# Other token blocks, another DMA model in the order planner, and first weight chunks halved by rows, in a two-layer decoder kernel on 8 cores

## The chip, the cores and the metric

The kernel runs on all 8 NeuronCores of one Trainium2 chip. Each core takes one prompt sequence (2048 tokens) and 16 of the 128 sample sequences (8 tokens each, 128 tokens in all), through both layers; nothing passes between cores. The weights are the same for all cores and each core reads them in f32 from HBM. The metric is the time on the device, in microseconds (us), of the slowest core. Engines: PE multiplies, ACT evaluates functions and copies, DVE does elementwise work, POOL does some of it and issues the weight DMAs, SP issues the other DMAs.

## The reference

Each layer normalises the tokens, multiplies them by one wide input matrix, and feeds three branches:

```python
hn = rms_norm(h, norm_mix)
proj = hn @ w_in
q, k, v, g_out, g_lr, xp, u, vv, gates = jnp.split(proj, offs, axis=-1)
g_log = log_sigmoid(g_lr @ w_gk2 + b_gk) / 16            # A: gated linear attention (GLA), 4 heads
o, s_new = gla_mix(q, k, v, g_log, s_gla, chunk)          # S_t = diag(a_t) S_{t-1} + k_t v_t ; o_t = q_t S_t
branch_a = (rms_norm(o, gla_norm) * silu(g_out)) @ w_br_a
branch_b = pool_mix(xp, ...) @ w_br_b                     # B: trailing means over 2, 4, 8, 16 tokens
branch_c = (gelu(u) * (tril(W_s) gelu(vv) + b)) @ w_br_c  # C: spatial gate in chunks of 128
h = h + (sigmoid(ga)*branch_a + sigmoid(gb)*branch_b + sigmoid(gc)*branch_c) @ w_out
h = h + relu(rms_norm(h) @ w_ff1)**2 @ w_ff2
```

D_MODEL is 1024, D_FF 4096; the outputs are the final-normed tokens, the GLA states, the pooling histories and the new v rows.

## The kernel before

**Tiles and blocks.** The 2176 tokens of a core are 17 tiles of 128. Tile 0 holds the sample tokens, tiles 1 to 16 the prompt. `BLK` (line 24) groups them in five blocks, here of 3, 3, 3, 4 and 4 tiles. A product with a weight chunk that is held feature-major (`hn_fm`, line 738) streams a whole block, so one matmul has 384 or 512 columns; one that is held token-major (`proj_tm`, `vgrp`) has a tile as the stationary operand and streams weight columns.

**Weight chunks.** The matrices come as chunks of 1024 x 512 (2 MB of f32 in HBM, 1 MB of bf16 in SBUF), in the fixed list `order`: v0, v1, k, q, g0, g1, xp, u, vv, and so on, through a ring `wring` of 7 slots. `wload` (line 651) issues them from POOL. The first two chunks, v0 and v1, come in two halves each, with semaphores of their own (`first`), and layer 0's `vgrp` starts on a half.

**Start.** x tiles come through three buffers `xt`, from SP. For each, ACT sums the squares (`xj`) and takes ln and exp for the root, DVE scales into `xn`, PE transposes, and DVE copies into `hn` (`norm_to_hn`, line 757). From tile 6 on, the load of x waits for chunk g0 (`after=[slots[4]]`).

**Stages.** In each layer: projections, gate and scan of the GLA branch block by block (`gla_project`, `gla_gate`, `gla_scan`), with the work on the 16 sample states cut into four portions by `yield` (line 990) and one portion after each of the first blocks; then pooling and spatial gate (`mix_block`), gated merge (`gate_block`), output projection (`out_block`), and the feed-forward net (`ff1`, `ff2`).

**ACT's tables.** Exp and ln share one table set; silu, gelu and sigmoid have one each (`SETS`, line 32). A switch shows in the profile as ACT_TABLE_LOAD.

**The order.** Nothing runs in the order of the code. Each operation is recorded as a node with a cost; `lay_out` (line 247) is a list scheduler that places nodes on five engines by its own clock, picks by start time and rank, and gives each PSUM tile a bank. DMA transfers end by a model of their own (`dma_at`). The instructions are then written in that order, and each engine runs its list strictly in turn. What the model believes of a duration changes only the order; the chip decides the times.

## Time and profile before

| | us |
|---|---|
| median of 3 runs | 2383.77 (2382.52 to 2385.54) |
| the profiled execution, its own time | 2381.28 |
| its span on the slowest core (core 5) | 2380.2 |
| spans of the other cores | 2371.6 to 2379.2 |
| PE busy | 2323.0 |
| DVE, ACT, POOL busy | 1273.8, 886.3, 245.9 |

The page divides the span into 40 slices of 59.5 us: PE is at 6 and 8 tenths in the first two and at 9 or more from the third to the last but one. The granted clock of PE averages 0.998 of full speed on this core. The GLA stages of the two layers lie at about 68 to 316 us and 1225 to 1480 us, and there ACT and DVE are at their busiest.

### The profile page before, as it was taken

What the parts mean: (1) busy time and instruction counts of PE and PEld (TensorE: products, weight loads), DVE (VectorE), ACT (ScalarE), POOL (GpSimd) and SP (SyncE); (2) the same over time, 40 slices, a digit from 0 to 9 for tenths busy, and PEclk for the clock granted to TensorE, in tenths of its full rate; (3) what the DMA queues carried; (4) which work ended last, traced back from release to release, by engine and by line L of the source; (5) the groups of instructions that cost most, each with busy time, mean ns of one, the idle gap of its engine ahead of it and who ended that gap; (6) DMA issues with size and microseconds to landing.
All of it is one profiled execution on the core that took longest, in us unless ns stands there. A gap on an engine that the chain in (4) does not pass through costs nothing.

```text
span 2380.2 us, 40912 instructions; the slowest of 8 cores (2371.6 to 2380.2 us)
## 1 busy us (share of the span) xinstructions
PE 2323.0 (98%) x13392; PEld 1236.5 (52%) x13392; DVE 1273.8 (54%) x2231; ACT 886.3 (37%) x1810; POOL 245.9 (10%) x266
## 2 busy tenths in 40 slices
PE   6899999999999999999999999999999999999998
PEld 4576555546445454545455555564554454545453
DVE  3787776444465444434567776744434644434355
ACT  3877753222233121212456678322222421211133
POOL 2123222000000000000012233200000000000000
PEclk9999999999999999999999999999999999999999
DMA  9554936154186040406492467451815642222112
GB/s 162 143 165 122 186 125 142 71 97 111 70 159 103 1 72 1 76 1 116 127 164 74 149 137 157 100 135 63 142 72 107 126 65 36 36 37 36 18 59 93
DMA packets 219415, 229.41 MB, mean 96 GB/s; under 512 B 54315, under 2 KB 203307, under 8 KB 216106
## 3 DMA queue, kind: packets, MB, share of 16 engines
q0 software_dynamic: 83584, 78.45, 23.8%
q1 hardware_dynamic: 135626, 148.35, 20.9%
q8 instruction: 113, 1.85, 0.3%
q14 instruction: 92, 0.75, 0.1%
HBM read 240.41 MB, written 55.05 MB: 124 GB/s over the span
## 4 chain that ended last, share of the span: by engine, by line
PE 91%; DVE 3%; issue 2%; ACT 2%; DMA 2%; POOL 0%; DVEq 0%; ACTq 0%; SPq 0%; POOLq 0%
PE ps L454 90%; DMA wring<-w_in 1%; PE ps L467 1%; DVE U L428 0%; DMA Sf<-sgla 0%; DVE Sf L428 0%; ACT rsg L417 0%; DVE tmp L428 0%; ACT L417 0%; ACT tmp L417 0%; DVE sqg L425 0%; DVE lv L815 0%; ACT Sb L417 0%; DVE pt L425 0%; ACT xj L417 0%
## 5 line engine op out<-in xcount | busy, mean ns | idle before, releaser
L454 PE MATMUL ps<-hn,wring 128*128 128x384 bf16 (+1 forms) x6400 | 1245.4, 347 | 7.8 <-DVE sgt L425 1.7
L454 PEld LDWEIGHTS ps<-hn,wring 128*128 128x128 bf16 x6400 | 621.6, 98 | 545.4 <-issue 13.4
L454 PE MATMUL ps<-wring,a 128*128 128x512 bf16 x2176 | 476.0, 379 | 0.2 <-DVE a L425 0.2
L417 ACT ACTIVATE rl<-ps 128x384 f32<-128x384 f32 (+1 forms) x320 | 169.9, 532 | 637.9 <-PE ps L454 522.2
L425 DVE TENSOR_TENSOR h<-h,ps 128x512 f32<-128x512 f32 x340 | 233.1, 687 | 277.1 <-PE ps L454 276.1
L454 PEld LDWEIGHTS ps<-wring,a 128*128 128x128 bf16 x2176 | 212.8, 98 | 255.1 <-issue 0.7
L425 DVE TENSOR_TENSOR a<-rl 128x384 bf16<-128x384 f32 (+1 forms) x320 | 194.9, 612 | 276.0 <-ACT rl L417 268.0
L417 ACT ACTIVATE sg<-ps 128x384 f32<-128x384 f32 (+1 forms) x240 | 127.9, 533 | 450.3 <-PE ps L454 322.3
L454 PE MATMUL ps<-wring,hn 128*128 128x256 bf16 (+1 forms) x1088 | 193.7, 330 | 12.2 <-DMA wring<-w_in 10.8
L425 DVE TENSOR_TENSOR tmp<-sg,ps 128x384 f32<-128x384 f32 (+1 forms) x160 | 97.3, 608 | 154.4 <-ACT sg L417 79.1
L454 PEld LDWEIGHTS ps<-wring,hn 128*128 128x128 bf16 x1088 | 105.2, 99 | 79.3 <-issue 15.3
L454 PE MATMUL ps<-OBs,wring 128*128 128x384 bf16 (+1 forms) x640 | 143.8, 347 | 0.0
L675 POOL DMA_DIRECT2D wring<-w_ff x32 | 28.0, 875 | 1047.2 <-PE ps L454 1047.2
L425 DVE TENSOR_TENSOR acc<-sg,ps 128x384 f32<-128x384 f32 (+1 forms) x80 | 48.5, 607 | 162.7 <-PE ps L454 162.7
L454 PE MATMUL ps<-H4s,wring 128*128 128x384 bf16 (+1 forms) x640 | 130.7, 347 | 0.0
L454 PE MATMUL ps<-wring,mg 128*128 128x512 bf16 x544 | 119.7, 379 | 0.0
L425 POOL TENSOR_TENSOR go<-tmp,go 128x512 bf16<-128x512 f32 x64 | 77.8, 1221 | 244.4 <-DVE tmp L428 213.0
L417 ACT ACT_TABLE_LOAD x71 | 91.1, 1283 | 26.4 <-PE ps L454 24.2
L454 PEld LDWEIGHTS ps<-H4s,wring 128*128 128x128 bf16 x640 | 62.5, 98 | 55.7 <-issue 0.3
L454 PEld LDWEIGHTS ps<-OBs,wring 128*128 128x128 bf16 x640 | 62.6, 98 | 55.0
L454 PEld LDWEIGHTS ps<-wring,mg 128*128 128x128 bf16 x544 | 52.8, 98 | 61.3
L428 DVE SCALAR_TENSOR_TENSOR tmp<-ps,vec_t,rsg 128x256 f32<-128x256 f32 x136 | 61.7, 477 | 28.6 <-ACT rsg L417 27.5
(137 smaller groups left out, 1777.6 us busy)
## 6 DMA issues: line engine op xcount, KB each, us to landing
wring<-w_ff POOLq DMA_DIRECT2D x32, 1024.0 KB, 13.1
wring<-w_in POOLq DMA_DIRECT2D x28, 1024.0 KB, 16.1
Sf<-sgla SPq DMA_DIRECT2D x64, 256.0 KB, 3.7
gla_s<-Sf SPq DMA_DIRECT2D x64, 256.0 KB, 2.8
H4s<-H_d SPq DMA_DIRECT2D x12, 768.0 KB, 8.5
OBs<-OB_d SPq DMA_DIRECT2D x12, 768.0 KB, 5.0
h_d<-h SPq DMA_DIRECT2D x17, 512.0 KB, 2.7
h<-h_d SPq DMA_DIRECT2D x17, 512.0 KB, 9.9
```

Source lines behind the costliest of these rows:

```text
L417: op(ACT, lambda: nc.scalar.activation(out=now(out), in_=now(in_), func=func, **kw), reads, writes, occ, 125.0, SETS.get(func))
L425: op(E, lambda: E.e.tensor_tensor(out=now(out), in0=now(in0), in1=now(in1), op=alu), reads, writes, occ, 90.0)
L428: op(DVE, lambda: nc.vector.scalar_tensor_tensor(out=now(out), in0=now(in0), scalar=scalar, in1=now(in1), op0=op0, op1=op1), reads, writes ...
L454: inst = nc.tensor.matmul(now(m[0]), m[1], m[2], start=m[3], stop=m[4], **kw)
L467: inst = nc.tensor.transpose(now(o), i, ident_ap)
L675: nc.gpsimd.dma_start(out=view, in_=src).then_inc(slot_sem[k], 16)
```

## The change

The kernel after has the blocks 4, 3, 4, 3, 3. The halves of v0 and v1 are cut by rows (four of the eight groups of 128 rows, all 512 columns) instead of by columns (all rows, 256 columns): a half product adds half of the sum into the same PSUM tile. Both chunks are issued ahead of the two small weights `wglr` and `wgk2`; `wglr` comes from HBM already padded to 32 columns, so that its memset is gone. The loads of `bsp` and `rep` follow tile 5 of `hn`; one more x tile (tile 6) is loaded without waiting for g0. The portions of the samples end at states 8, 18 and 28 instead of 6, 16 and 26. The product of the pooling weights (`fuse`) is recorded inside the first gate block rather than ahead of it. The planner's DMA model now lets the transfers of both queues progress together, at 300 and 265 bytes per ns, and frees what waits for a transfer when it lands by that model.

```diff
 NTILE = 17
-BLK = [(0, 3), (3, 3), (6, 3), (9, 4), (13, 4)]
+BLK = [(0, 4), (4, 3), (7, 4), (11, 3), (14, 3)]
...
     w_gk2 = din("w_gk2", [DEPTH, 128, 512])
-    w_glr = din("w_glr", [DEPTH, 128, KT, 16])
+    w_glr = din("w_glr", [DEPTH, 128, KT, 32])
...
-        dma_at = [4000.0] * 5
+        clock = 4000.0
+        coming = []
+        moving = {3: collections.deque(), 4: collections.deque()}
+        landing = []
...
                     best = pick
+            upto = best[1] if best is not None else 1e12
+            while clock < upto and (coming or moving[3] or moving[4]):
+                on = [(moving[3], 3.0 if moving[4] else 1.0), (moving[4], 1.5 if moving[3] else 1.0)]
+                on = [(q, r) for q, r in on if q]
+                to = min([upto] + [clock + q[0][1] * r for q, r in on] + ([max(clock, coming[0][0])] if coming else []))
+                for q, r in on:
+                    q[0][1] -= (to - clock) / r
+                    if q[0][1] < 1e-6:
+                        m = q.popleft()[0]
+                        landing.append((to + m.lat, m.idx))
+                        landing.sort()
+                clock = to
+                while coming and coming[0][0] <= clock:
+                    _, i, e, work = coming.pop(0)
+                    moving[e].append([nodes[i], work])
+                if landing and landing[0][0] < upto:
+                    upto = landing[0][0]
+            if landing and landing[0][0] <= upto:
+                at, i = landing.pop(0)
+                free_up(nodes[i], at)
+                continue
...
             if n.byts:
-                at0 = max(dma_at[e], s + occ)
-                other = dma_at[7 - e]
-                work = n.byts / (290.0 if e == 3 else 150.0 if dma_at[4] < 20000.0 else 245.0)
-                both = max(0.0, other - at0)
-                dma_at[e] = at0 + (both + work - both / 2 if work > both / 2 else work * 2)
-                fin = dma_at[e] + (3500.0 if e == 3 else 2500.0)
+                coming.append((s + occ, n.idx, e, n.byts / (300.0 if e == 3 else 265.0) + 100.0))
+                coming.sort()
...
                 n *= s
-            if turn:
-                n *= 3
-            record(self.E, fn, reads, writes, 500.0 if self.E is SP else 900.0, 0.0, byts=n, after=after)
+            record(self.E, fn, reads, writes, 1250.0 if turn else 500.0 if self.E is SP else 900.0,
+                   2000.0, byts=n, after=after)
...
     hH = [[part(hB[t], 0, 2 * KB), part(hB[t], 2 * KB, 2 * KB)] for t in range(NTILE)]
-    mkb = [24, 30, 36, 42, 50]
+    mkb = [24, 32, 38, 46, 52]
...
             for i in range(2):
-                c = slice(256 * i, 256 * i + 256)
-                plq.dma(vs[0][:, :, c], todo[0][1][:, :, c], writes=[first[2 * n + i]])
+                c = slice(4 * i, 4 * i + 4)
+                plq.dma(vs[0][:, c, :], todo[0][1][:, c, :], writes=[first[2 * n + i]])
...
             release((slot_sem[k], 16 * slot_cnt[k]), rs, ws)
-        record(POOL, fn, (), [b] + (first[2 * k:2 * k + 2] if n in (NSLOT, NSLOT + 1) else []), 900.0 * len(todo), 0.0, byts=byts)
+        record(POOL, fn, (), [b] + (first[2 * k:2 * k + 2] if n in (NSLOT, NSLOT + 1) else []), 900.0 * len(todo), 2000.0, byts=byts)
...
         act(ssq[7].t[:, :], ssq[7].t[:, :], AF.Ln, [ssq[7]], [ssq[7]])
-        memset(wglr.t[:, :, :], 0.0, [wglr])
...
     def gla_consts(l):
-        plq.dma(wglr.t[:, :, 0:16], w_glr[l], writes=[wglr])
+        plq.dma(wglr.t[:, :, :], w_glr[l], writes=[wglr])
             ts(wpm.t[:, g, :], wpm.t[:, g, :], vec_t.t[:, V_PSC + l * 4 + g:V_PSC + l * 4 + g + 1], ALU.mult, [wpm, vec_t], [wpm])
-        spq.dma(bsp.t[:, :, :], b_sp[l:l + 1].broadcast_to([128, 4, 128]), writes=[bsp], after=[slots[6]])
+        spq.dma(bsp.t[:, :, :], b_sp[l:l + 1].broadcast_to([128, 4, 128]), writes=[bsp], after=[hnB[5]])
         plq.dma(wsT.t[:, :, :], w_spT[l].rearrange("g s t -> s g t"), writes=[wsT], after=[slots[6]])
-        spq.dma(rep.t[:, :], rep_d[l], writes=[rep], after=[slots[6]])
+        spq.dma(rep.t[:, :], rep_d[l], writes=[rep], after=[hnB[5]])
...
                 for i in range(2):
-                    c = slice(256 * i, 256 * i + 256)
-                    pe_group([(ps.t[:, c], hn_v(b)[:, kt, j * 128:(j + 1) * 128], view[:, kt, c], kt == 0, kt == KT - 1, True)
-                              for kt in range(KT)], [first[2 * hf + i], hnB[BLK[b][0] + j]], [ps])
+                    pe_group([(ps.t[:, :], hn_v(b)[:, kt, j * 128:(j + 1) * 128], view[:, kt, :], kt == 0, kt == KT - 1, True)
+                              for kt in range(4 * i, 4 * i + 4)], [first[2 * hf + i], hnB[BLK[b][0] + j]], [ps])
...
                 spq.dma(gla_s[l, i, 2 * hp:2 * hp + 2].rearrange("h d e -> d h e"), s.t[:, :, :], reads=[s])
-                if n in (5, 15, 25):
+                if n in (7, 17, 27):
...
         ga, ba, gb, bbc, gc = [wget(l, "%s%d" % (nm, hf)) for nm in ("ga", "ba", "gb", "bbc", "gc")]
-        if b == 0:
-            for g in range(4):
-                ps = psum()
-                pe_group([(ps.t[:, :], wpm.t[:, g, :], bbc[1][:, g, :], True, True)], [wpm, bbc[0]], [ps])
-                act(bbc[1][:, g, :], ps.t[:, :], AF.Copy, [ps], [bbc[0]])
+        def fuse(g):
+            ps = psum()
+            pe_group([(ps.t[:, :], wpm.t[:, g, :], bbc[1][:, g, :], True, True)], [wpm, bbc[0]], [ps])
+            act(bbc[1][:, g, :], ps.t[:, :], AF.Copy, [ps], [bbc[0]])
                 m = hf * 4 + m4
+                if b == 0 and pi == 0 and m4 > 1:
+                    fuse(2 * m4 - 4)
+                    fuse(2 * m4 - 3)
...
         for t in tiles(b):
-            norm_to_hn(t, hB[t].t[:, :], hH[t], hj, hx[t % 2], turn=b >= 2)
+            norm_to_hn(t, hB[t].t[:, :], hH[t], hj, hx[t % 2], turn=t > 5)
...
     for t in range(NTILE):
-        if t == 6:
+        if t == 7:
             wget(0, "g1")
-        spq.dma(xt[t % 3].t[:, :], rows(x_p, x_s, t), writes=[xt[t % 3]], after=[slots[4]] if t > 5 else ())
+        spq.dma(xt[t % 3].t[:, :], rows(x_p, x_s, t), writes=[xt[t % 3]], after=[slots[4]] if t > 6 else ())
...
                 act(wn.t[:, i * 512:(i + 1) * 512], wps[i].t[:, :], AF.Copy, [wps[i]], [wn])
-            wget(0, "v0")
+            wget(0, "v1")
...
     gk2 = gk2.reshape(DEPTH, 128, 512)
-    glr = np.ascontiguousarray(f(w_in)[:, :, C_GLR:C_GLR + 16].reshape(DEPTH, KT, 128, 16).transpose(0, 2, 1, 3))
+    glr = np.zeros((DEPTH, 128, KT, 32), np.float32)
+    glr[:, :, :, 0:16] = f(w_in)[:, :, C_GLR:C_GLR + 16].reshape(DEPTH, KT, 128, 16).transpose(0, 2, 1, 3)
     shared = {
```

**PE at the start**, from the first product with v0 on. xn are tiles being transposed. dq_pl0 to dq_pl5 are the POOL queue's first transfers in the order of issue: before, v0's halves, wglr, wgk2, v1's halves; after, v0's halves, v1's halves, wglr, wgk2. Before:

```order
L454 MATMUL ps<-wring,hn 128x256 [waits dq_pl0,sem_dve]
L454 MATMUL ps<-wring,hn 128x256 x7
L467 MATMUL ps<-ident_bf,xn_71 128x128 [waits sem_dve]
L467 MATMUL ps<-ident_bf,xn_71 128x128 x7
L454 MATMUL ps<-wring,hn 128x256 [waits sem_dve]
L454 MATMUL ps<-wring,hn 128x256 x7
L467 MATMUL ps<-ident_bf,xn_70 128x128 [waits sem_dve]
L467 MATMUL ps<-ident_bf,xn_70 128x128 x7
L454 MATMUL ps<-wring,hn 128x256 [waits dq_pl1]
L454 MATMUL ps<-wring,hn 128x256 x15
L454 MATMUL ps<-hn,wglr 32x384 [waits dq_pl2,sem_dve]
L454 MATMUL ps<-hn,wglr 32x384 x7
```

After:

```order
L480 MATMUL ps<-wring,hn 128x512 [waits dq_pl0,sem_dve]
L480 MATMUL ps<-wring,hn 128x512 x3
L480 MATMUL ps<-wring,hn 128x512 [waits dq_pl1]
L480 MATMUL ps<-wring,hn 128x512 x3
L493 MATMUL ps<-ident_bf,xn_71 128x128 [waits sem_dve]
L493 MATMUL ps<-ident_bf,xn_71 128x128 x7
L480 MATMUL ps<-wring,hn 128x512 [waits dq_pl2]
L480 MATMUL ps<-wring,hn 128x512 x3
L480 MATMUL ps<-wring,hn 128x512 [waits sem_dve]
L480 MATMUL ps<-wring,hn 128x512 x11
L493 MATMUL ps<-ident_bf,xn_70 128x128 [waits sem_dve,sem_act]
L493 MATMUL ps<-ident_bf,xn_70 128x128 x7
```

Tile 0 now takes both halves of v0 before tile 1 is transposed, and a product with the first half of v1 (dq_pl2) stands ahead of tile 1's own products.

**ACT in the GLA stage of layer 0**, at the gate of the first block that it works on with 512 columns after block 0; go are silu results, rsg needs ln and exp. Before:

```order
L417 ACTIVATE tmp_0_96<-ps 128x512
L417 ACTIVATE go_78<-ps 128x512 x2
L417 ACTIVATE rsg_98<-ps 128x256
L417 ACTIVATE rsg_98<-rsg_98 128x256
L417 ACTIVATE go_78<-ps 128x512 x2
L417 ACTIVATE tmp_1_97<-ps 128x512
L417 ACTIVATE Sb_90<-U_86,eblP 128x256
L417 ACTIVATE Sb_91<-U_87,eblP 128x256
L417 ACTIVATE go_78<-ps 128x512
L417 ACTIVATE tmp_0_96<-ps 128x512
L417 ACTIVATE rsg_99<-ps 128x256
L417 ACTIVATE rsg_99<-rsg_99 128x256
```

After:

```order
L443 ACTIVATE rsg_98<-ps 128x256
L443 ACTIVATE rsg_98<-rsg_98 128x256
L443 ACTIVATE go_77<-ps 128x512 x2
L443 ACTIVATE Sb_90<-U_86,eblP 128x256
L443 ACTIVATE Sb_91<-U_87,eblP 128x256
L443 ACTIVATE tmp_1_97<-ps 128x512
L443 ACTIVATE Sb_92<-U_88,eblP 128x256
L443 ACTIVATE Sb_93<-U_89,eblP 128x256
L443 ACTIVATE tmp_0_96<-ps 128x512
L443 ACTIVATE go_77<-ps 128x512 x6
L443 ACTIVATE rsg_99<-ps 128x256
```

Before, the silu results come in twos and ones with rsg between them; after, six of them stand in one row.

## Rows read from the trace of the kernel before

**Rows 1.** First two lines of the page, core 5: engine, busy us, share.

```profile
span 2380.2 us, 40912 instructions; the slowest of 8 cores (2371.6 to 2380.2 us)
...
PE 2323.0 (98%) x13392; PEld 1236.5 (52%) x13392; DVE 1273.8 (54%) x2231; ACT 886.3 (37%) x1810; POOL 245.9 (10%) x266
```

**Rows 2.** Busy time by stage; columns PE, PEld, DVE, ACT, POOL, clock, DMA share, GB/s.

```profile
30.00:43.00 13.00, 8.15 (x60) 6.03 (x58) 4.54 (x8) 6.72 (x19) 0.00 (x0) 0.74 1.13 151
68.00:125.00 57.00, 50.14 (x417) 33.59 (x415) 42.11 (x74) 47.55 (x115) 7.35 (x6) 1.00 0.52 147
125.00:250.00 125.00, 118.44 (x1051) 82.23 (x1049) 103.43 (x240) 95.43 (x188) 43.44 (x51) 1.00 0.51 139
250.00:316.00 66.00, 63.11 (x432) 36.12 (x430) 48.83 (x106) 51.39 (x101) 20.94 (x21) 1.00 0.86 169
1225.00:1480.00 255.00, 244.17 (x1753) 141.57 (x1752) 184.45 (x417) 189.92 (x380) 69.41 (x74) 1.00 0.54 125
```

**Rows 3.** Waits of PE: total us, times, longest.

```profile
PE ps L454 <- DMA wring<-w_in: 10.8, 3, 4.9
```

**Rows 4.** PE in order of time, 14 to 60 us: start, length, operation.

```profile
17.73 1.86 PE L454 MATMUL ps<-wring,hn 128*128 128x256 bf16 x8 [4.67 <-DMA wring<-w_in]
...
24.47 1.91 PE L454 MATMUL ps<-wring,hn 128*128 128x256 bf16 x16 [1.27 <-DMA wring<-w_in]
...
36.43 5.16 PE L454 MATMUL ps<-wring,hn 128*128 128x256 bf16 x24 [4.85 <-DMA wring<-w_in]
...
41.87 3.66 PE L454 MATMUL ps<-wring,hn 128*128 128x256 bf16 x32
45.37 0.61 PE L467 MATMUL ps<-ident_bf,xn 128*128 128x128 bf16 x8
...
51.05 5.36 PE L454 MATMUL ps<-hn,wring 128*128 128x384 bf16 x32
```

**Rows 5.** DMA, 20 to 25 us.

```profile
DMA packets 1672, 1.11 MB, mean 223 GB/s; under 512 B 967, under 2 KB 1482, under 8 KB 1672
...
q0 software_dynamic: 1450, 0.34, 77.3%
```

**Rows 6.** DMA, 28 to 34 us.

```profile
DMA packets 1669, 1.21 MB, mean 201 GB/s; under 512 B 298, under 2 KB 1570, under 8 KB 1668
...
q0 software_dynamic: 1163, 0.62, 82.1%
```

**Rows 7.** DMA, 50 to 60 us.

```profile
q0 software_dynamic: 1524, 1.53, 111.8%
```

**Rows 8.** Instructions on tile xt, 0 to 140 us: duration ns min/median/max.

```profile
L417 ACT ACTIVATE xj<-xt x17: 1039/1055/1074, 5.6 to 113.4; 128x1024 bf16<-128x1024 f32 x17
L417 ACT ACTIVATION_READ_ACCUMULATOR xj<-xt x17: 185/187/219, 6.5 to 114.3; 128x1 f32 x17
L428 DVE SCALAR_TENSOR_TENSOR xn<-xt,ssq,wn x17: 1273/1280/1286, 10.6 to 120.0; 128x1024 bf16<-128x1024 f32 x17
```

**Rows 9.** DVE in order of time: the copy of a transposed tile.

```profile
31.52 0.69 DVE L437 COPY hn<-ps 128x1024 bf16<-128x1024 bf16 x1 [2.91 <-PE ps L467]
```

**Rows 10.** SP queue in order of time, 0 to 130 us.

```profile
3.99 0.47 SPq L379 DMA_DIRECT2D bsp_p<-b_spatial  x1
```

**Rows 11.** ACT groups, 68 to 316 us: busy us, mean ns, idle before.

```profile
L417 ACT ACT_TABLE_LOAD x31 | 39.8, 1283 | 7.2 <-PE ps L454 6.8
```

**Rows 12.** ACT groups, 1225 to 1480 us.

```profile
L417 ACT ACT_TABLE_LOAD x32 | 41.1, 1283 | 15.6 <-PE ps L454 15.2
```

**Rows 13.** Line L417 over the whole span.

```profile
L417 ACT ACT_TABLE_LOAD  x71: 1283/1283/1283, 1.3 to 1856.7; - x71
```

**Rows 14.** Chain that ended last: shares by line, then two of its pieces.

```profile
by line: PE ps L454 89.9%; issue 2.1%; DMA wring<-w_in 1.3%; PE ps L467 0.7%; DVE U L428 0.4%; DMA Sf<-sgla 0.4%; DVE Sf L428 0.3%; ACT rsg L417 0.3%; DVE tmp L428 0.3%; ACT L417 0.3%; ACT tmp L417 0.3%; DVE sqg L425 0.2%; DVE lv L815 0.2%;
...
42.04 3.49 PE ps L454 x32
...
699.47 1.73 PE ps L454 x8
```

More of the change, by code:

```diff
@@ L1 @@
+import collections
 import numpy as np
@@ L270, in lay_out, with free_up @@
                 ready[num[id(n.E)]].append(n)
-        for _ in range(len(nodes)):
+        def free_up(n, fin):
+            for m in n.succ:
+                j = m.idx
+                t = fin + 250.0 if n.E is not PE or m.E is not PE else fin - n.lat
+                if t > rdy[j]:
+                    rdy[j] = t
+                need[j] -= 1
+                if need[j] == 0:
+                    ready[num[id(m.E)]].append(m)
+        while len(order) < len(nodes):
             while oldest < len(tiles_in_order) and id(tiles_in_order[oldest]) in opened:
@@ L336, in lay_out @@
             order.append(n)
-            for m in n.succ:
-                j = m.idx
-                t = fin + 250.0 if e != 0 or m.E is not PE else fin - n.lat
-                if t > rdy[j]:
-                    rdy[j] = t
-                need[j] -= 1
-                if need[j] == 0:
-                    ready[num[id(m.E)]].append(m)
+            if not n.byts:
+                free_up(n, fin)
         return max(free), order, kof
```

## The prediction

> **What bounds the kernel now.** I read the page's busy shares first [rows 1]: PE is busy for 2323.0 of 2380.2 us. The change touches no product's size, only when it runs, so what can be won is PE's idle time and what PE loses inside its busy time. The table by stage [rows 2] shows where that lies. PE idles 57 - 50.1 = 6.9 us from 68 to 125 us, 6.6 from 125 to 250, 2.9 from 250 to 316, and 10.8 in layer 1's GLA stage. That is 16.3 us in layer 0's stage and 27.1 in both; ACT is busy for 47.6 of 57 us in the first of these stretches. The rest is the start. PE's waits [rows 3] put 10.8 us there on three waits for chunks of w_in, and PE's own order of time [rows 4] shows them: v0's first half at 17.7 us, v1's first half at 36.4. From 41.9 us on PE runs without a gap to 68.
>
> **The start.** What must arrive ahead of v1's first half gets smaller, and I price it per packet. From 28 to 34 us, when the POOL queue moves halves by columns, its 1163 packets took 82.1% of 16 x 6 = 96 us: 67.8 ns each, and 0.62 MB / 1163 is about 512 B [rows 6]. From 50 to 60 us, with whole chunks, 1524 packets took 111.8% of 160 us: 117.4 ns for 1024 B [rows 7]. A half by columns is 1024 packets, 69.4 us of engine time or 4.34 us over 16 engines; by rows it is 512 packets, 60.1 us or 3.76. Three halves save 1.7 us. w_glr was 1024 packets of 32 B: from 20 to 25 us 1450 packets took 77.3% of 80 us, and if the 483 that are not under 512 B cost 67.8 ns, the other 967 cost 30 ns [rows 5]; so w_glr is 1.9 us. w_gk2 is 128 packets of 1024 B, 0.9 us. Both now come behind v1. bsp (0.26 MB, issued at 4.0 us [rows 10]) now comes after tile 5; at the 201 GB/s of [rows 6] 1.3 us. The masks (0.17 MB) wait for tile 2, which comes later, 0.8. x tile 5 (0.52 MB, 2.6 at that rate) is asked for some 4 us later; I take 0.6 of it. Sum: 7.2 us, so v1's first half lands at 36.4 - 7.2 = 29.2 us.
>
> The trace agrees only in part with the Trainium skill (DMA: Bandwidth & Descriptors, Specifications), which says that transfers of 512 B and more already run at line rate. By that rule the cut by rows gives nothing, v1 lands 1.7 us later than I say, and the predicted time is 1.7 us higher. The packets above cost 0.132 ns per byte at 512 B and 0.115 at 1024 B, so I go by them.
>
> PE's list, though, gives much of this back. After v1's first half lands it runs: 16 products of 512 columns; the transposes of tile 2 and their copy; 8 and 12 products; tile 3's transposes; 4 products; wglr; 8 products. A product costs 216 ns at full clock (8 in 1.73 us) [rows 14]. PE has by then stood idle, as before 36.4 us, where 24 products of 256 columns took 5.16 us, 215 ns each against 3.49 / 32 = 109 [rows 4, 14], with a granted clock of 0.74 over 30 to 43 us [rows 2]: the lower level, 1.2 GHz, after 5 us of waiting. I let 8 of the 16 run at it: 8 x 0.43 + 8 x 0.216 = 5.2 us. The transposes and copy are 0.5 + 0.7 [rows 9], 20 products 4.3, transposes 0.5, 4 products 0.9, wglr 0.4, 8 products 1.7: 14.2, with 0.3 for waits between. That is a state 0.3 us of work short of what the kernel before has reached at 45.4 us (52 products' worth of 512 columns there, 56 here, but two sets of transposes and gates fewer). So the start breaks even if v1 lands at 45.4 - 14.8 = 30.6, and gains 1.4 us at 29.2. Bounds: with packets and w_gk2 alone (2.6 us) it loses 3.2; with all of x tile 5 out of the way (9.2 us) it gains 3.4. I take 1.4, since nearly all of the 7.2 has rows.
>
> ACT and DVE stand behind PE here: ACT now copies v of tile 0 before it sums tile 2's squares, and v of tile 1 before tile 3's. Tile 3's chain (1.06 + 0.19 + 0.5 on ACT, 1.28 on DVE [rows 8]) starts when tile 1's product is done, about 3.5 us after v1's landing, and ends near 8.5, while its transposes stand at 10.8. It is covered by 2 us. From k on the chunks are not late: PE reaches k's first product near 50 us, and before it found k there at 51.05 without a wait [rows 4].
>
> **The GLA stages.** A table load costs ACT 1283 ns, and there are 71 [rows 13], 31 in layer 0's stage and 32 in layer 1's [rows 11, 12]. I counted, in ACT's list of each kernel, the changes between the sets of exp/ln, silu, gelu and sigmoid. Before gives 71, the trace's number. After gives 52: 14 fewer in layer 0, 5 fewer in layer 1, because silu results stand together in longer runs. That is 24.4 us less on ACT. What PE gets of it: on the chain that ended last, ACT's table loads are 0.3% of 2380, 7.1 us for 71, or 0.1 us each [rows 14]; 19 give 1.9. From above: if all of PE's idle time in these stages came from loads, 14 x 16.3/31 + 5 x 10.8/32 = 9.1. Below, an order in which other operations take the place of the loads gives 0. I take 3.0, nearer to the chain, since it is the row that follows releases.
>
> One x tile more (tile 6) is normed before the crowded stretch: 11 were normed there with 6.9 us of idle PE, so 0.6. PE's halves: 272 products of 512 columns stand for 544 of 256: 272 x (2 x 109 - 216) = 0.5.
>
> **Edits at nothing.** wglr's memset ran on DVE before the first x arrived. The fuse products, the yields, `mkb` and the turn rule keep their counts (tiles 6 to 16 are turned as before); they lie in stretches where PE is full. h of tile 16 now shares space with block 2 and 3 of the merge and is loaded 2 tiles ahead instead of 3, 2 x 16 x 0.216 = 6.9 us before use; its adds wait on DVE and PE has free PSUM banks. The blocks keep their number, and three of 384 columns and two of 512 stay. The last block is of 3 tiles, which shortens only ACT's 0.6 us step there. As bounds for all reordering beside the loads I keep 4 us either way, 15% of the 27.1.
>
> **Sum.** 1.4 + 3.0 + 0.6 + 0.5 = 5.5 us off the profiled execution's 2381.3 gives 2375.8. The median of the runs is 2.5 above that execution, so 2383.8 - 5.5 = 2378.3 us.
>
> **Rivals.** A measurement tells 0.2%, 4.8 us, from no change.
> A, the forecast: 2 to 9 us faster, 2375 to 2382. Chance 0.50, of which 0.30 beyond the bound.
> B, the table loads count nearly in full: ACT is over 80% busy from 68 to 125 us [rows 2], and waits on it pass to PE through DVE. 9.1 for 3.0, and 2 more at the start: 13.6 faster, 2370. Against it: the chain holds few loads. 0.18.
> C, nothing: v1 lands at 30.6 and ACT's saved time turns into waits for PE. The trace shows ACT's loads already preceded by 15.6 us of idling in layer 1 [rows 12]. 0.5 + 0.6 = 1.1 faster, 2382.7. 0.19.
> D, slower: PE's clock. The waits for v0's second half and v1's first stand close together, and PE has 4 products and one set of transposes between them. If it stays at 1.2 GHz through all 48 products behind v1's landing, 40 more than I count, that costs 40 x 0.216 = 8.6 us; with the loads at their lower bound: -1.4 - 1.1 + 8.6 = 6.1 slower, 2389.9. It decides from 34 of the 40 on. For it: the 24 products at 36.4 us all ran low. Against it: the next 32, from 41.9 us, all ran at full clock [rows 4]. 0.13.
> That the change doesn't do what it says has no place beside the counted loads and packets.
>
> The likeliest is A, 2378.3. The range 2367 to 2387 holds A and C, most of B, and the better edge of D. Faster 0.30 + 0.18 = 0.48, the same 0.20 + 0.19 = 0.39, slower 0.13.
>
> **What the profile after would show.** POOL packets of 1024 B from the start; PE's first product on v1 at 28 to 31 us, and tile 4's transposes near 44; 52 table loads; PE's idle time in the two GLA stages down from 27 to about 24 us; a granted clock at the low level for 2 to 4 us around 30 us. I am wrong if v1 lands after 32 us, if PE waits on k or q, or if the GLA stages idle as before with 19 loads fewer.

## The result, and the profile after

The kernel after takes 2397.2 us (median of 5 runs, 2392.9 to 2398.0), that of before 2383.8 (5 runs, 2380.9 to 2385.5): the ratio is 1.005, 95% interval 1.0036 to 1.0063. The forecast was 2378.3, with 2367 to 2387 as its range and 0.13 for slower: the measured time lies 10 us above the range. In some executions cores of one die run at a lower clock, whatever the kernel; the ratios leave these out, except for one execution of a_turn3 (2414.5 us), one of a_nudge (2411.5) and two of b_blkyield (2415.7 and 2423.7), without which theirs are given too.

The profiled execution took 2398.0 us; its slowest core is core 0. First the head of its page, to be held against [rows 1]:

```profile
span 2397.0 us, 40156 instructions; the slowest of 8 cores (2381.0 to 2397.0 us)
...
PE 2321.9 (97%) x12948; PEld 1212.1 (51%) x13120; DVE 1277.8 (53%) x2230; ACT 861.6 (36%) x1791; POOL 247.6 (10%) x266
```

PE is as busy as before, and stands idle for 75.1 us where it was 57.2. (Part of that is not idling: 172 matmul records are missing from this core's trace, as 12948 stand beside 13120 weight loads.) Busy time also hides something, which the table by stage shows in its clock column (core 0; columns as in [rows 2]):

```profile
30.00:43.00 13.00, 11.12 (x67) 5.33 (x70) 4.64 (x5) 7.78 (x19) 0.00 (x0) 1.00 1.12 200
68.00:125.00 57.00, 50.84 (x386) 29.70 (x387) 48.06 (x88) 45.92 (x115) 9.89 (x8) 0.96 0.54 135
125.00:250.00 125.00, 117.34 (x874) 67.59 (x883) 98.54 (x219) 88.53 (x180) 39.35 (x46) 1.00 0.43 125
250.00:316.00 66.00, 54.88 (x359) 31.74 (x360) 40.57 (x94) 42.67 (x95) 20.98 (x21) 0.90 1.07 203
1225.00:1480.00 255.00, 245.14 (x1711) 140.35 (x1731) 181.22 (x406) 185.34 (x382) 68.11 (x74) 1.00 0.62 133
```

From 250 to 316 us PE idles 11.1 us for 2.9, and the granted clock averages 0.90 for 1.00. Before, it had been 1.00 in every stretch from 68 us on.

One core is one sample, so I took the same stretches on all eight. This table is worked out from them: the mean of PE's idle time, and of what the clock cost (the stretch times one minus its mean granted clock), in us.

| stretch | before: idle, clock | after: idle, clock | change |
|---|---|---|---|
| 0 to 68 us | 17.3, 2.1 | 19.2, 0.7 | +0.5 |
| 68 to 380, to the end of layer 0's mixing | 17.0, 0.0 | 18.9, 6.2 | +8.1 |
| 740 to 860, output projection, then ff1 and ff2 | 0.1, 0.0 | 2.7, 0.8 | +3.4 |
| 1225 to 1540, the same mixing in layer 1 | 11.2, 0.0 | 8.7, 0.0 | -2.5 |
| 1900 to 2360, layer 1's feed-forward | 0.7, 0.0 | 2.6, 0.0 | +1.9 |

The sum is +11.4 us; the mean span of the eight cores went from 2376.0 to 2387.3. So the table leaves nothing large out, and the loss has two places: layer 0's mixing, mostly by PE's clock, and the two feed-forward stages. The clock column has two digits, which makes its products rough: the falls in the trace itself, 3.4 or 6.8 us each at 0.50, add up to 5.6 us for the 6.2. And it misses something in the first row of the table: up to a core's first clock record (20 to 27 us before, 22 to 31 after) it says 1.00 while 4 products of 512 columns take 1.86 us, 465 ns each, half speed. Estimated as half of PE's busy time up to there, this cost 5.2 us before and 6.1 after.

**The start** brought v1 earlier than forecast. PE of core 0 in order of time, beside [rows 4]:

```profile
15.69 1.86 PE L480 MATMUL ps<-wring,hn 128*128 128x512 bf16 x4 [3.23 <-DMA wring<-w_in]
21.98 1.86 PE L480 MATMUL ps<-wring,hn 128*128 128x512 bf16 x4 [4.43 <-DMA wring<-w_in]
...
25.92 3.61 PE L480 MATMUL ps<-wring,hn 128*128 128x512 bf16 x16 [1.22 <-DMA wring<-w_in]
...
31.24 4.26 PE L480 MATMUL ps<-wring,hn 128*128 128x512 bf16 x19 [1.26 <-ACT ssq L443]
...
39.85 0.61 PE L493 MATMUL ps<-ident_bf,xn 128*128 128x128 bf16 x8 [0.50 <-DVE xn L454]
...
45.47 1.89 PE L480 MATMUL ps<-hn,wring 128*128 128x512 bf16 x8
```

v1's first product is at 25.9 us, not 29.2. The 16 products take 3.61 us here, 226 ns each, which is full clock; on the other seven cores they take 5.3 to 6.1 us. Core 1 of the same execution, and core 2 of the kernel before, which [rows 4] (core 5) should be held against:

```profile
25.92 5.62 PE L480 MATMUL ps<-wring,hn 128*128 128x512 bf16 x16 [3.97 <-DMA wring<-w_in]
```

```profile
30.39 2.78 PE L454 MATMUL ps<-wring,hn 128*128 128x256 bf16 x24 [2.76 <-DMA wring<-w_in]
```

Before, PE's first product with v1 was at 30.4 to 36.4 us, by core, 32.9 in the mean; core 5 was the last. Now it is at 24.9 to 26.4, 25.8 in the mean. ACT loads as many tables as counted, 52 for 71:

```profile
L443 ACT ACT_TABLE_LOAD x52 | 66.7, 1283 | 32.6 <-PE ps L480 30.6 <-DVE ssq L467 1.3
```

**The clock.** The largest single wait of core 0, and what follows it; first PE in order of time, then the table by stretches:

```profile
257.12 1.46 PE L480 MATMUL ps<-hn,wring 128*128 128x384 bf16 x8
...
264.68 0.24 PE L480 MATMUL ps<-kqS,Sinb 128*128 128x8 bf16 x4 [5.99 <-POOL Sinb L463]
...
265.19 2.76 PE L480 MATMUL ps<-hn,wring 128*128 128x384 bf16 x8
...
268.07 6.56 PE L480 MATMUL ps<-hn,wring 128*128 128x384 bf16 x32
```

```profile
258.00:262.00 4.00, 0.69 (x5) 0.23 (x3) 1.78 (x4) 2.28 (x7) 0.00 (x0) 1.00 1.03 168
262.00:266.00 4.00, 1.32 (x9) 0.85 (x10) 0.43 (x2) 0.00 (x0) 1.72 (x2) 0.71 1.12 201
266.00:270.00 4.00, 4.00 (x15) 1.78 (x13) 3.07 (x8) 1.54 (x4) 1.15 (x2) 0.50 1.08 224
270.00:274.00 4.00, 4.00 (x25) 2.36 (x24) 3.53 (x6) 1.33 (x3) 2.03 (x3) 0.94 1.02 286
```

Eight products of 384 columns take 1.46 us ahead of the wait and 2.76 behind it. The clock column shows 0.50, the 1.2 GHz level; the engine had stood nearly idle for six us. "PE busy" says 4.00 of 4.00 us there: a fall of the clock is invisible in busy shares. The wait is paid a second time behind itself. It also happened without a long wait: core 1 has only waits of 0.4 to 1.1 us, but five of them from 284 to 292 us, and then PE runs at the low level:

```profile
284.00:288.00 4.00, 2.95 (x26) 1.58 (x23) 2.98 (x7) 1.99 (x7) 2.27 (x2) 1.00 1.09 156
288.00:292.00 4.00, 1.49 (x13) 0.84 (x13) 2.83 (x9) 3.81 (x10) 0.00 (x0) 1.00 1.14 160
292.00:296.00 4.00, 2.99 (x13) 1.85 (x14) 1.43 (x4) 3.21 (x9) 2.31 (x2) 0.60 1.12 158
296.00:300.00 4.00, 4.00 (x12) 1.53 (x11) 2.01 (x4) 2.30 (x8) 0.95 (x1) 0.54 1.13 210
```

**The feed-forward stages.** Before, PE waited for nothing between 740 and 860 us. Now it waits for DVE's squares `a`. Three rows of DVE, two views of SP's queue (732 to 738 us and 750 to 755), and one row of PE, all of core 0:

```profile
761.91 1.28 DVE L454 SCALAR_TENSOR_TENSOR hx<-h,ssq,wn 128x1024 bf16<-128x1024 f32 x1 [4.62 <-DMA hn<-hx]
763.11 1.29 DVE L451 TENSOR_TENSOR a<-rl 128x512 bf16<-128x512 f32 x2
768.28 1.28 DVE L454 SCALAR_TENSOR_TENSOR hx<-h,ssq,wn 128x1024 bf16<-128x1024 f32 x1 [3.88 <-DMA hn<-hx]
```

```profile
L406 SPq DMA_TRANSPOSE hn<-hx x2: 1231/1232/1232, 732.5 to 734.3; - x2
...
DMA to landing us min/median/max: 3.0/3.0/3.0
```

```profile
L406 SPq DMA_TRANSPOSE hn<-hx x2: 1238/2760/4282, 751.4 to 753.5; - x2
...
DMA to landing us min/median/max: 10.4/12.6/14.7
```

```profile
771.73 0.81 PE L480 MATMUL ps<-wring,a 128*128 128x512 bf16 x3 [1.67 <-DVE a L451]
```

DVE scales a tile into one of two buffers `hx`, and SP transposes it by DMA into `hn`. DVE can't write the buffer until the transpose has read it. The two transposes of 732.5 and 734.3 us each landed 3.0 us after their issue. Those of 751.4 and 753.5 us, issued while two weight chunks of 1 MB from POOL were under way (issued at 751.2 and 752.9, landed at 761.2 and 768.0), took 10.4 and 14.7 us, and at their landings, 761.8 and 768.2, DVE's two waits above end. DVE's strict order has the scaling ahead of the squares, so the squares stand behind a DMA that they don't need, and PE behind the squares.

### The profile page after: what moved, and what is told of

Its sections match the earlier page's. It is cut to its first block, busy times and chain, and to the rows that moved or that the text cites. A ratio compares the mean times of both kernels' runs of the same rounds, so it can differ in the third digit from the quotient of the medians.

```text
span 2397.0 us, 40156 instructions; the slowest of 8 cores (2381.0 to 2397.0 us)
## 1 busy us (share of the span) xinstructions
PE 2321.9 (97%) x12948; PEld 1212.1 (51%) x13120; DVE 1277.8 (53%) x2230; ACT 861.6 (36%) x1791; POOL 247.6 (10%) x266
## 4 chain that ended last, share of the span: by engine, by line
PE 87%; DMA 5%; DVE 3%; issue 2%; ACT 2%; POOL 1%; SPq 0%; DVEq 0%; ACTq 0%; POOLq 0%
PE ps L480 87%; DMA hn<-hx 1%; DMA Sf<-sgla 1%; DMA wring<-w_in 1%; DMA H_d<-go 1%; PE ps L493 1%; ACT L443 0%; DVE tmp L454 0%; DMA rep<-w8rep 0%; ACT rsg L443 0%; POOL go L451 0%; DVE Sf L454 0%; DVE U L454 0%; DVE xn L454 0%; DVE km L458 0%
## 5 line engine op out<-in xcount | busy, mean ns | idle before, releaser
L480 PE MATMUL ps<-wring,hn 128*128 128x512 bf16 x786 | 185.0, 381 | 13.8 <-DMA wring<-w_in 8.9
L480 PEld LDWEIGHTS ps<-wring,hn 128*128 128x128 bf16 x816 | 77.6, 98 | 98.7 <-issue 17.2
## 6 DMA issues: line engine op xcount, KB each, us to landing
wring<-w_ff POOLq DMA_DIRECT2D x32, 1024.0 KB, 11.2
H4s<-H_d SPq DMA_DIRECT2D x12, 768.0 KB, 5.0
OBs<-OB_d SPq DMA_DIRECT2D x12, 768.0 KB, 5.1
```

Source lines behind the costliest of these rows:

```text
L480: inst = nc.tensor.matmul(now(m[0]), m[1], m[2], start=m[3], stop=m[4], **kw)
```

## The experiments

All kernels below are this kernel with some parts of the change. Beside the ratio to the kernel before I read three numbers from the trace, as means over the eight cores: when ACT does its first gate of `gate_block` in layer 0 (380.9 us before, 389.3 after: "first gate"), the time from the first to the last relu in layer 0's feed-forward (453.8 with the blocks of before, 456.5 with the new ones where nothing waits), and layer 1's first gate to the end (832.5).

**Which part costs?** The start alone, the blocks alone, the planner's DMA model alone, and all but the planner's model:

b_start has the lines of the start (row halves, both chunks first, the padded w_glr, bsp and rep behind tile 5, x tile 6 earlier):

```diff
-                c = slice(256 * i, 256 * i + 256)
-                plq.dma(vs[0][:, :, c], todo[0][1][:, :, c], writes=[first[2 * n + i]])
+                c = slice(4 * i, 4 * i + 4)
+                plq.dma(vs[0][:, c, :], todo[0][1][:, c, :], writes=[first[2 * n + i]])
...
-            wget(0, "v0")
+            wget(0, "v1")
```

> The kernel before with the start of the kernel after alone: row halves, both first chunks ahead of the small weights, the padded w_glr, bsp and rep behind tile 5, x tile 6 loaded without waiting. Blocks, planner, sample portions and fuse are those of before. Theory P (the planner's new DMA model causes the loss) and theory B (the new blocks cause it): 0 to 4 us faster than before, 2380 to 2384 us. Theory S (the start causes it: v1 comes earlier but the rest of the start loses what it gives, and puts DVE's work later): 5 to 13 us slower, 2389 to 2397.

Measured: 1.0028 (1.0016 to 1.0039), first gate at 386.8 us.

b_blocks:

```diff
-BLK = [(0, 3), (3, 3), (6, 3), (9, 4), (13, 4)]
+BLK = [(0, 4), (4, 3), (7, 4), (11, 3), (14, 3)]
...
-    mkb = [24, 30, 36, 42, 50]
+    mkb = [24, 32, 38, 46, 52]
```

> The kernel before with the blocks 4, 3, 4, 3, 3 alone, with the places in SBUF of the merge buffers that go with them. Theory B (a first block of four tiles crowds DVE from 80 to 125 us, where it went from 33.7 to 42.4 us busy of 45, and PE's clock falls there): 8 to 13 us slower, 2392 to 2397 us. Theory P and theory S: within 3 us of before.

Measured: 1.0156 (1.0137 to 1.0175), first gate at 398.8, and 21.8 us more between the two first gates.

b_plan has all lines on the planner's DMA model; a_oldplan is the kernel after without them:

```diff
-                dma_at[e] = at0 + (both + work - both / 2 if work > both / 2 else work * 2)
-                fin = dma_at[e] + (3500.0 if e == 3 else 2500.0)
+                coming.append((s + occ, n.idx, e, n.byts / (300.0 if e == 3 else 265.0) + 100.0))
+                coming.sort()
...
-            if turn:
-                n *= 3
-            record(self.E, fn, reads, writes, 500.0 if self.E is SP else 900.0, 0.0, byts=n, after=after)
+            record(self.E, fn, reads, writes, 1250.0 if turn else 500.0 if self.E is SP else 900.0,
+                   2000.0, byts=n, after=after)
```

> The kernel before with the planner's new DMA model alone. Theory P (it takes a DMA transpose for a cheap transfer, puts DVE's work that waits for one too early, and plans the landings of state and weights too early): 6 to 13 us slower, 2390 to 2397 us, with waits of PE on DVE of 2 to 4 us in the feed-forward stages near 770 and 1930 us. Theory B and theory S: within 3 us of before.

Measured: 1.0147 (1.0130 to 1.0164), first gate at 404.4, feed-forward 460.7 for 453.8, last part 839.0 for 832.5.

> The kernel after with the planner's DMA model of before; the blocks, the start, the portions and the fuse are those of after. Theory P: the loss goes, 2378 to 2385 us, below before. Theory B or S: it stays, 2392 to 2398 us. If the parts only work together (theory M: any new order loses or wins by chance some us), this lies between.

Measured: 1.0069 (1.0054 to 1.0084), first gate at 394.4; the feed-forward stages run as if nothing waited (456.4, 832.0).

Each of the three parts alone costs, two of them three times as much as all together. (The later fuse and the sample portions were not run alone.) Each theory of one guilty part falls. Only the feed-forward waits follow a part, the planner's model.

**The transpose's price, and the other parts undone one by one.**

a_turn3 is the kernel after with one line changed; a_oldblk and a_oldstart are the kernel after without the lines of b_blocks and of b_start.

```diff
-                   2000.0, byts=n, after=after)
+                   2000.0, byts=3 * n if turn else n, after=after)
```

> The kernel after; alone the planner again counts the bytes of a DMA transpose three times, as before (issue and delay stay as after). Theory P1 (the planner takes the transposes of the feed-forward stage for too cheap and puts the scaling of the next tile ahead of the squares that PE waits for): PE's waits on DVE at about 760 to 775 and 1930 us go, 2.4 + 0.9 us in the first and 2.0 in the last stage, so the ratio to the kernel before falls from 1.005 to about 1.003 (2391 to 2393 us). Rival (any change of the planner's numbers shuffles the whole order): the stages ahead of 380 us change too, by up to 8 us either way.

Measured: 1.0051, with a wide interval (1.0021 to 1.0081); without the execution of 2414.5 us 1.0023, which is what the theory had. The trace is clear: feed-forward 456.5 for 460.0, last part 832.4 for 835.0, the first gate 1.1 us later (390.4), mean span 2382.6 for 2387.3. The mean of the cores' spans lies at 2381.7 to 2383.5 in the four other executions, and at 2385.0 to 2387.3 in all five of the kernel after.

> The kernel after with the blocks 3, 3, 3, 4, 4 and their buffers of before; start, planner, portions and fuse are those of after. Theory B (blocks of four tiles first bring the fall of PE's clock): the ratio to before falls below 1.002. Theory F (the parts are fitted to each other: each alone cost 3 to 37 us, together 12): it rises to 1.010 to 1.016, like the planner alone.

Measured: 1.0103 (1.0087 to 1.0118).

> The kernel after with the start of before (halves by columns, small weights between the first two chunks, bsp and rep behind g0's slot, one x tile fewer). Theory S (the start costs what b_start showed, 0.28%): the ratio to before falls from 1.005 to 1.002. Theory F: it rises, to 1.007 or more.

Measured: 1.0036 (1.0022 to 1.0051). k's first product comes 4.6 us later than in the kernel after (54.3 for 49.7, by DVE's copy of its result), and yet the first gate is 3.8 us earlier (385.5).

b_blkyield is b_blocks and:

```diff
-                if n in (5, 15, 25):
+                if n in (7, 17, 27):
```

> The kernel before with the new blocks and the new ends of the sample portions. Theory F in its plainest form: a first block of four tiles gives its portion of samples more time, and with the portions of before PE waits for the states of the samples (7.3 us on POOL's Sinb at 262 and 301 us with the blocks alone). Then the ratio falls from 1.0156 with the blocks alone to 1.008 or less, and those waits to under 3 us. Rival: the portions do nothing, 1.014 to 1.017.

Measured: 1.0097 (1.0068 to 1.0125), 1.0073 without the executions of 2415.7 and 2423.7 us. The profiled one is that of 2415.7, so I read it without its cores 2 and 3, which stood at 0.98 in the mean. The first gate of the other six is at 398.9, as late as with the blocks alone, and the clock cost 8.3 us from 68 to 380; the gain over the blocks alone came from layer 1.

**Do the two parts add up, and what does any other order cost?** b_rows has the halves by rows, their order and the padded w_glr only. a_turn3_oldstart is a_turn3 with the start of before.

> The kernel after with two parts undone: the planner counts the bytes of a DMA transpose three times, and the start is that of before. If the two parts add up: the transposes gave back 4.8 us of the mean span (2387.3 to 2382.5, the feed-forward waits gone), the start 3.8 us ahead of the first gate (389.3 to 385.5): mean span 2378.7 us, first gate at 385.5, ratio to before 1.000 to 1.003. Theory F (parts only fit together, each change shuffles the whole order): the first gate anywhere from 381 to 393 us. The waits in the feed-forward stages are gone by either.

Measured: 0.9996 (0.9984 to 1.0008), first gate at 383.8, mean span 2375.6. I could have stopped here: two parts undone, the time of before is back.

> The kernel before with the row halves, both first chunks ahead of the small weights and the padded w_glr alone; bsp, rep and the x tiles are loaded as before. What b_start cost (0.28%, first gate at 386.8 us for 380.9, although the first half of v1 came earlier) lies either in bsp, rep and the x tile moved ahead, then this is 0.998 to 1.001, or in what follows the rows (the small weights late, one product group of 512 columns), then it is 1.002 to 1.004 as b_start.

Measured: 1.0030 (1.0019 to 1.0041). k's first product is 1.7 us earlier than before (47.0 for 48.7), the first gate 6.3 us later (387.2).

b_turn1 is the kernel before with two lines less:

```diff
-            if turn:
-                n *= 3
```

> The kernel before; alone the planner no longer counts a DMA transpose three times. Theory P1: PE waits on DVE's squares at about 770 and 1930 us come up here too, some 2 to 5 us each with the clock falling there, and the rest stays as before: ratio 1.002 to 1.005. Rival: the rest of the planner's model is needed for it, then the feed-forward stages idle as before (0.1 and 0.7 us) and the ratio is 1.000.

Measured: 1.0076 (1.0062 to 1.0089). The first gate stayed (380.7). Feed-forward and last part: 461.7 for 453.8, 839.3 for 832.5. The rows that decide it, on core 4 of this kernel, DVE and then PE:

```profile
744.61 0.56 DVE L423 TENSOR_TENSOR a<-rl 128x384 bf16<-128x384 f32 x1 [0.74 <-ACT rl L415]
755.46 1.28 DVE L426 SCALAR_TENSOR_TENSOR hx<-h,ssq,wn 128x1024 bf16<-128x1024 f32 x1 [10.30 <-DMA hn<-hx]
756.67 1.02 DVE L423 TENSOR_TENSOR a<-rl 128x384 bf16<-128x384 f32 x2
```

```profile
759.86 12.93 PE L452 MATMUL ps<-wring,a 128*128 128x512 bf16 x47 [6.84 <-DVE a L423]
```

The kernel before, DVE at the same place (core 5): more squares stand between the scalings, the buffer is nearly free when its turn comes, and PE waits for none of it.

```profile
746.54 1.28 DVE L428 SCALAR_TENSOR_TENSOR hx<-h,ssq,wn 128x1024 bf16<-128x1024 f32 x1 [0.41 <-DMA hn<-hx]
748.28 0.56 DVE L425 TENSOR_TENSOR a<-rl 128x384 bf16<-128x384 f32 x1 [0.46 <-ACT rl L417]
...
755.29 1.28 DVE L428 SCALAR_TENSOR_TENSOR hx<-h,ssq,wn 128x1024 bf16<-128x1024 f32 x1 [1.25 <-DMA hn<-hx]
```

b_nudge is the kernel before with every landing of a DMA 250 ns later in the model:

```diff
-                fin = dma_at[e] + (3500.0 if e == 3 else 2500.0)
+                fin = dma_at[e] + (3750.0 if e == 3 else 2750.0)
```

> The kernel before; alone each DMA lands 250 ns later in the planner's model, a change with no meaning for the chip. It measures what any other order of the same work costs. Theory F (the order of before is a lucky one of many, and any other loses some us to waits and to falls of PE's clock in layer 0's GLA stage): the first gate comes 3 to 12 us later than at 380.9 us, ratio 1.002 to 1.006, and the clock falls once or twice between 60 and 340 us, where it never did before. If the order of before is ordinary, this lies within 1 us of it.

Measured: 1.0050 (1.0037 to 1.0064), first gate at 390.3; idle 24.5 us and clock 2.3 from 68 to 380. A change that means nothing costs as much as the whole change under study.

**Cost or luck?** If a quarter of a microsecond in the model can do that, no single pair of kernels tells what the start costs. So each was nudged: b_nudge_back by -250 ns, b_rows_nudge, a_turn3_nudge, a_turn3_oldstart_nudge and a_nudge by +250, a_turn3_nudge500 by +500. In the kernels with the new model the line is:

```diff
-                        landing.append((to + m.lat, m.idx))
+                        landing.append((to + m.lat + 250.0, m.idx))
```

> The kernel before; alone each DMA lands 250 ns earlier in the planner's model. A second draw beside the nudge of +250 ns, which cost 0.5%. If the order of before is a lucky one: ratio 1.002 to 1.006 again, the first gate 3 to 12 us after 380.9. If only later landings hurt: 0.998 to 1.001.

Measured: 1.0126 (1.0111 to 1.0141), first gate at 411.1. Waits of PE on core 4, 250 to 400 us, the three longest kinds:

```profile
PE ps L454 <- POOL Sinb L437: 5.4, 2, 3.1
PE ps L454 <- ACT xf L417: 5.3, 2, 5.1
PE ps L454 <- DVE sgt L425: 3.8, 2, 2.5
```

> The kernel before with row halves (as b_rows, 1.003) and the nudge of +250 ns (alone 1.005). If the rows themselves cost 0.3% whatever the order: 1.008. If their cost is that of any other order (luck): they don't add up, 1.000 to 1.006.

Measured: 1.0057 (1.0042 to 1.0072), against 1.0050 with the same nudge without rows.

> The kernel after with transposes counted three times (1.0051 with a wide interval, mean span 2382.5 us) and every landing 250 ns later in the planner's model. If the start of after costs whatever the order: 1.002 to 1.005, and 3 to 5 us above the same nudge with the start of before. If luck: 0.998 to 1.008, with no fixed distance to it.

Measured: 0.9987 (0.9977 to 0.9996), median 2381.1 us. First gate at 378.3. Its feed-forward stages on core 1, and the kernel after's on the same core, 740 to 860 us:

```profile
740.00:860.00 120.00, 120.00 (x605) 58.99 (x603) 51.70 (x80) 22.43 (x43) 3.50 (x4) 1.00 0.36 51
```

```profile
740.00:860.00 120.00, 118.18 (x596) 57.86 (x594) 50.86 (x78) 23.83 (x47) 3.23 (x4) 1.00 0.32 49
```

> The same as a_turn3_oldstart (0.9996), with every landing 250 ns later in the planner's model. If blocks and planner of after are as good as those of before by themselves: 0.998 to 1.002 again. If 0.9996 was a lucky order: 1.002 to 1.006, as the nudge did to before. Below 0.998 it would be a version that beats both kernels.

Measured: 1.0037 (1.0022 to 1.0051), first gate at 387.7.

> The kernel after (transposes cheap, as it is); alone every landing is 250 ns later in the planner's model. With transposes counted three times the same nudge gave 0.9987. If cheap transposes cost 5 us under any order (PE waits on DVE's squares near 760 and 1930 us): 1.0007 to 1.002, with these waits there. If that too belongs to single orders: anything from 0.998 to 1.010, and the waits may be gone.

Measured: 1.0031 (1.0005 to 1.0058), 1.0020 without the execution of 2411.5 us; first gate at 379.0. Its feed-forward (459.9) and last part (835.0) are those of the kernel after; a_turn3_nudge has 456.4 and 832.0.

> The kernel after with transposes counted three times and every landing 500 ns later (0 ns: 1.0051 with a wide interval; 250 ns: 0.9987). If the gain at 250 ns comes with any later landing: 0.997 to 0.9995. If it was one lucky order: 1.001 to 1.007.

Measured: 0.9999 (0.9988 to 1.0011), first gate at 380.9, 45 table loads.

What the pairs say, the ratio with and without each part, all else the same; a_turn3 and a_nudge stand without the executions named:

| part | pairs, with against without | reading |
|---|---|---|
| transposes priced low | after 1.0050 / 1.0023 (mean span 2387.3 / 2382.6); nudged 1.0020 / 0.9987; on before 1.0076 / 1.0000 | costs in every pair: 6.1, 6.5 and 14.7 us in the feed-forward stages |
| the new start | on before 1.0028 / 1.0000; after 1.0050 / 1.0036; with a_turn3 1.0023 / 0.9996; nudged 0.9987 / 1.0037 | +0.28, +0.14, +0.27 and -0.50%: no cost of its own is shown |
| the new blocks | on before 1.0156 / 1.0000; after 1.0050 / 1.0103 | +1.6 and -0.5% |
| the new planner's model | on before 1.0147 / 1.0000; after 1.0050 / 1.0069 | +1.5 and -0.2% |
| row halves | on before 1.0030 / 1.0000; nudged 1.0057 / 1.0050 | +0.3% and +0.07% |
| nudge alone | before: 1.0050 and 1.0126; after: 1.0050 to 1.0020; a_turn3: 0.9987, 0.9999 for 1.0023; a_turn3_oldstart: 1.0037 for 0.9996 | moves the first gate by 4 to 30 us |

## Why the prediction was wrong

**The step that failed** is the one called "Edits at nothing", with its bound: "As bounds for all reordering beside the loads I keep 4 us either way, 15% of the 27.1." I took that bound as a share of PE's idle time, as if a new order could only redistribute what was idle. The nudges show what the same work costs in another order: on the kernel before the first gate moved by 9 us and by 30, where the bound had 4. The kernel before is a good order for its first 380 us: from 68 us to 2360 no core shows a fall of the clock. The kernel after has its first gate 8.4 us later, and with a nudge, all its parts in place, at 379.0, earlier than before.

**In the same step**, "the turn rule keep their counts ... they lie in stretches where PE is full" is wrong in its conclusion. The count of transposed tiles did stay. The diff also takes away `n *= 3`, which stood in front of me as a number that "changes only the order". The order was what kept DVE's squares ahead of a slow DMA. Priced by bytes the transfer of a tile of 256 KB (128 x 1024 of 2 bytes) went from 2.7 us in the model to 1.0. With the model's other terms (1.25 for the issue, 2.0 at the end, the transfer three times as long while POOL's queue moves) a tile beside weights lands 6.2 us after its issue in the new model, and by the line of a_turn3 11.4; on core 0 such tiles took 10.4 and 14.7. So the factor 3 is close where a weight chunk is under way, and too dear for a tile that has the engines to itself: 6.0 in the model of a_turn3, 3.0 measured. That the cheap price makes the waits is shown, in three pairs, and it is the only part of the loss that has a cause in one line: 6.1 us in the mean, of 11.3.

The Trainium skill (Advanced Engine Details and Errata, X-Bar Transpose (TRN2)) says that transposing DMAs are as fast as regular ones, at 350 to 400 GB/s. By that a tile would take 0.7 us, an estimate from the page's figure. This trace does not agree: the lone tile of core 0 that was issued at 732.5 us moved its 256 KB from 733.7 to 735.1, at a mean of 187 GB/s, and the measurement decides.

**The start, +1.4 forecast.** In the mean of the cores the stretch from 0 to 68 us lost 0.5 instead. The landing of v1 was sized well: PE's first product with it is 7.1 us earlier in the mean (25.8 for 32.9) for the 7.2 forecast, and the 16 products behind it took 5.3 to 6.1 us on seven of eight cores, for the 5.2 forecast. What the sum had wrong was the core that it started from: core 5, the last of the eight to get v1. By DVE's copy of k's first result, core 5 gained 3.7 us (49.3 for 53.0) and core 2 lost 5.1 (49.6 for 44.5); the mean went from 48.7 to 49.7. With rows alone k's came 1.7 us earlier, and idle plus clock from 0 to 68 us fell from 19.4 to 17.0 us. But k's first product is not where time is banked: a_oldstart reached it 4.6 us later and the first gate 3.8 us earlier.

**The table loads, +3.0 forecast.** The count was exact, the gain is not there in layer 0. From 68 to 380 us idle plus clock is 17.0 us with 71 loads in the whole kernel (before), 17.5 with 71 (b_turn1), 47.1 with 71 (b_nudge_back), 25.1 with 52 (after), 18.4 with 45 (a_turn3_nudge500), 15.2 with 55 (a_turn3_nudge). There is no order in this. Layer 1's stage did lose 2.5 us of idle time; whether by its fewer loads is open, no run changed the loads alone.

**The rivals.** D came nearest: PE's clock, as a price paid behind clustered waits. It was right in kind: the falls cost 5.6 us in layer 0's mixing, and 5.4 more than before over the whole span, of the 11.3. But I looked for it only at 30 us, where waits for weights stand close. It struck near 66 us on two cores, near 100 on seven, and in layer 0's last blocks on all: at 264 and 305 us on core 0, behind one wait of 6 us and behind shorter ones, and at 292 to 296 on the other seven, behind several of 0.4 to 1.7. B is refuted. The terms of 0.6 and 0.5 us are below what these runs tell apart.

**What stays open.** Which feature makes an order good between 68 and 380 us was not found. Waits for the samples' states (POOL's Sinb, 5.99 us on core 0 and 1.9 in all on core 4 of the same execution) differ from core to core and count by the clock behind them too; no experiment took them away. That a later landing in the model is better in general is not shown either: +250 ns was better for a_turn3 and worse for a_turn3_oldstart and before.

The best of the orders is a_turn3_nudge: 0.9987 (0.9977 to 0.9996) of before, that is the change with the transposes priced three times and one lucky nudge, and it is the lowest of 19 tries.

## What to carry to other kernels

Where a list scheduler writes the order, treat any edit of its costs, or of its nodes, as a fresh draw: nudge a constant two or three times first, and let the range of the forecast, and every verdict on a part, be no narrower than that spread (here 0.2 to 1.3%). An edit that only changes what the planner believes of a duration has a price: find the instruction that the belief holds back or lets forward, and ask who is queued behind it on its engine. Add up PE's idle time and what its clock cost over all cores and stretches before naming a cause; busy shares alone would have shown half of this loss. And start a sum from the mean of the cores as well as from the slowest: the one that is last in the end need not be typical in the stretch that the change touches.

## What the runs showed of the hardware

A transposing DMA of one 128 x 1024 bf16 tile that had the engines to itself took 1.23 us of SP's queue, moved its bytes at 187 GB/s and landed 3.0 us after its issue (after, core 0, 732.5 us). Beside two weight chunks of 1 MB it landed 10.4 and 14.7 us after its issue (after, core 0), and 14.6 and 15.2 us in b_turn1 (core 4). PE's granted clock fell to 0.50 behind one wait of 5.99 us, and equally behind five waits of 0.4 to 1.1 us; the falls lasted 3.4 or 6.8 us, and cost half of that. Up to the first clock record of a core the profile's column says 1.00, while 512 columns take 465 ns. Cores with the same program end 16 us apart in one execution (2381.0 to 2397.0): the slowest core, which sets the time, was 4.2 us above the mean before (2380.2 for 2376.0) and 9.7 after (2397.0 for 2387.3).
